# Feed-forward products of a two-layer decoder step in blocks of seven products for eight

## The reference, cut to what matters

```
x += (gelu(causal_dwconv3(h2 @ w_u)) * (h2 @ w_g)) @ w_down,   h2 = RMSNorm(x)
D_MODEL = 1024, FFN_DIM = 2816, CONV_W = 3
w_up: (DEPTH, 1024, 2 * 2816) holds w_u and w_g; w_down: (DEPTH, 2816, 1024)
```

## Time and profile before

| | |
|---|---|
| runs | 2318.37, 2318.27 and 2322.32 us, median 2318.37 |
| profiled execution | span 2314.9 us, from the first to the last instruction; the page gives no time around the span |
| busy in the span | PE 98%, PE weight loads 79%, VectorE 35%, ScalarE 20%, GpSimd 7% |
| granted clock of PE | 0.994 of full, mean |
| feed-forward stage of layer 0 | from 669.83 to 1159.6 us; of layer 1 from 1815.9 us to the end |
| transfers | 237.50 MB, mean 103 GB/s |

### The profile page before, as it was taken

How to read it: one execution, slowest core, us unless ns; L and a number is a source line. 1 busy time by engine, 2 the same in 40 slices (tenths; PEclk the granted TensorE clock), 3 DMA queues, 4 the chain that set the end, 5 groups by cost and what they waited for, 6 DMA issues and landing times.

```text
span 2314.9 us, 29844 instructions
## 1 busy us (share of the span) xinstructions
PE 2266.4 (98%) x12615; PEld 1821.0 (79%) x12615; DVE 815.3 (35%) x1860; ACT 455.2 (20%) x957; POOL 154.9 (7%) x245
## 2 busy tenths in 40 slices
PE   8998999999999999999999989999999999999999
PEld 7787776788888888888877867767888888888887
DVE  5566646444133222100026565574421322222000
ACT  2123135321011111110012231354101111111000
POOL 5140010010000000000021300100100000000000
PEclk9999999999999999999999999999999999999999
DMA  6674621112222222222384726111222212222222
GB/s 181 220 247 164 243 85 37 37 59 93 76 73 73 73 73 70 64 53 68 81 275 129 258 92 273 55 37 37 96 73 76 73 63 68 70 73 64 66 75 76
DMA packets 195081, 237.50 MB, mean 103 GB/s; under 512 B 39807, under 2 KB 174464, under 8 KB 192192
## 3 DMA queue, kind: packets, MB, share of 16 engines
q1 hardware_dynamic: 176104, 133.11, 19.4%
q0 software_dynamic: 18400, 102.36, 11.9%
q10 hardware_dynamic: 444, 0.12, 0.0%
HBM read 222.76 MB, written 21.11 MB: 105 GB/s over the span
## 4 chain that ended last, share of the span: by engine, by line
PE 91%; DVE 3%; DMA 2%; ACT 2%; issue 1%; another core or an unknown queue 1%; SPq 0%; POOL 0%; DVEq 0%; ACTq 0%; POOLq 0%
PE PS L814 51%; PE PS L1455 14%; PE PS L926 5%; PE PS L836 4%; PE PS L862 3%; PE PS L1260 2%; PE PS L1177 2%; PE PS L1188 2%; PE PS L414 2%; DMA arena<-in_cache_kv_slc_dram,idx 2%; ACT arena L1486 1%; PE PS L1135 1%; DVE arena L2143 1%; PE PS L1160 1%
## 5 line engine op out<-in xcount | busy, mean ns | idle before, releaser
L814 PE MATMUL PS<-hT,ring 128*128 128x272 f32 x4352 | 1013.4, 395 | 5.8 <-issue 2.9
L814 PEld LDWEIGHTS PS<-hT,ring 128*128 128x128 f32 x4352 | 828.0, 191 | 185.1 <-issue 15.1
L1486 ACT ACTIVATE arena<-PS 128x512 f32<-128x512 f32 (+13 forms) x307 | 135.2, 475 | 1082.9 <-PE PS L814 559.8
L1455 PE MATMUL PS<-arena,ring 128*128 128x272 f32 x1408 | 323.7, 392 | 0.0
L1455 PEld LDWEIGHTS PS<-arena,ring 128*128 128x128 f32 x1408 | 267.2, 190 | 54.8
L1812 DVE TENSOR_TENSOR arena<-PS,arena 128x544 f32<-128x544 f32 (+3 forms) x124 | 75.4, 618 | 376.6 <-PE PS L814 319.1
L814 PE MATMUL PS<-arena,ring 128*128 128x272 f32 x768 | 177.2, 393 | 3.1 <-DVE arena L1812 3.1
L1818 DVE SCALAR_TENSOR_TENSOR arena<-arena,prm 128x32 f32<-128x32 f32 (+1 forms) x176 | 88.0, 500 | 249.2 <-ACT arena L1486 245.9
L814 PEld LDWEIGHTS PS<-arena,ring 128*128 128x128 f32 x768 | 145.8, 190 | 33.9 <-DVE arena L1812 4.0
L1812 DVE TENSOR_TENSOR xT<-PS,xT 128x544 f32<-128x544 f32 x32 | 23.2, 725 | 386.2 <-PE PS L1455 303.2
L836 PE MATMUL PS<-ring,hT 128*128 128x256 f32 x640 | 142.2, 381 | 0.6 <-ACT qT L1486 0.6
(11 more groups left out here) (311 smaller groups left out, 1620.5 us busy)
## 6 DMA issues: line engine op xcount, KB each, us to landing
ring<-in_w_up_dram SPq DMA_DIRECT2D x88, 512.0 KB, 4.1
ring<-in_w_in_dram SPq DMA_DIRECT2D x68, 512.0 KB, 4.7
ring<-in_w_down_dram SPq DMA_DIRECT2D x32, 384.0 KB, 3.6
ring<-in_w_down_dram SPq DMA_DIRECT2D x32, 320.0 KB, 4.3
arena<-in_state_kv_win_dram POOLq DMA_DIRECT2D x4, 2048.0 KB
ring<-in_w_out_dram SPq DMA_DIRECT2D x16, 512.0 KB, 4.3
out_dram<-in_state_kv_win_dram POOLq DMA_DIRECT2D x2, 4064.0 KB, 40.0
ring<-in_w_in_dram SPq DMA_DIRECT2D x16, 256.0 KB, 6.5
```

The costliest lines, as they stand in the source:

```text
L814: mm = pe.matmul(PS[0:m, b + a, 0:HALF], weight(k), rhs(k)[:, HALF * a:HALF * a + HALF], start=(k == 0), stop=(k == nk - 1))
L1455: mm = pe.matmul(PS[:, b + a, 0:HALF], w[:, k, :], aT[:, 11 * half + k, HALF * a:HALF * a + HALF], start=(half == 0 and k == 0), stop=(hal ...
L1486: return nc.scalar.activation(out, in_, func, **kw)
```

## The change

The matrix products of up/gate steps 1 to 10 and of the whole down stage are cut into blocks of 2 x 2: the input features in two halves (of 4 row blocks; in the last part of down of 3), the output features in two chunks of 128, the tokens in two halves of 272. Such a block took eight products of a quarter of the weights with a quarter of the tokens; now it takes seven, each of 4 (or 3) matmuls of 272 tokens. Four sums of weight quarters and four of token quarters are made on VectorE: the weight sums for every block (`weight_sum`, into `sums` and, one of them, in place in the ring), the token sums of `hT` once a layer (`hsum`, over the place of `raw`), those of `aT` once per pair of row blocks (`asum`, in the strips that attention and convolution have left free).

The seven products add onto each other in PSUM. Bank x of the first ticket is a running sum that is read four times (after its 1st, 2nd, 3rd and last product), bank z of the second ticket twice, bank z+1 once. TensorE waits (`taken`) before it adds onto a bank whose value is still to be read. In the up/gate loop ScalarE copies four partial results (`take`, `take_last`) and VectorE adds three (`add_seven`); in the down stage VectorE adds all seven to `xT`. The centre tap is now made from `ue`, and the gate is multiplied in from `aT`. The down stage runs in three parts over the hidden features (8, 8 and 6 row blocks), each over four pairs of output chunks, so that each pair of `xT` is added to three times. The last two chunks of the output are turned and stored together (before: the last alone).

```diff
+DOWN = [(8 * part, min(8, FC - 8 * part) // 2, pair) for part in range(3) for pair in range(KC // 2)]
+SEVENS = [f"{kind}{i}" for i in range(1, FFN // WCOLS) for kind in "ug"] + [f"d{n}" for n in range(len(DOWN))]
...
+            def half_product(bank, weight, rhs, kc, start, stop):
+
+                for k in range(kc):
+                    mm = pe.matmul(PS[:, bank, 0:HALF], weight[:, k, :], rhs(k), start=(start and k == 0), stop=(stop and k == kc - 1), skip_group_check=not start)
+                return mm
+
+            def seven_products(name, pool, first, second, kc, top, low, right, t1, t2, t3, t4, taken, between=None):
+
+                n, s = SEVEN_AT[name], wload(name)
+                new = sums[n % 2][:, :, 0:kc, :]
+                pe.wait_ge(*S.claim(pe, pool, first))
+                x = S.banks(pe, first)
+                half_product(x, quarter(s, kc, 0, 0), top, kc, True, True).then_inc(*S.inc(pe, "part"))
+                pe.wait_ge(*S.claim(pe, pool, second))
+                z = S.banks(pe, second)
+                pe.wait_ge(*S.at(pe, "w_sum", 4 * n + 1))
+                pe.wait_ge(*t1[0])
+                half_product(z, new[:, 0], t1[1], kc, True, True).then_inc(*S.inc(pe, "part"))
+                pe.wait_ge(*taken[0])
+                pe.wait_ge(*S.at(pe, "w_sum", 4 * n + 3))
+                pe.wait_ge(*t2[0])
+                half_product(x, new[:, 1], t2[1], kc, False, True).then_inc(*S.inc(pe, "part"))
+                half_product(z + 1, quarter(s, kc, 1, 0), low, kc, True, True).then_inc(*S.inc(pe, "part"))
+                pe.wait_ge(*taken[2])
+                pe.wait_ge(*t3[0])
+                half_product(x, quarter(s, kc, 0, 1), t3[1], kc, False, True).then_inc(*S.inc(pe, "part"))
+                pe.wait_ge(*taken[1])
+                pe.wait_ge(*S.at(pe, "w_sum", 4 * n + 4))
+                half_product(z, new[:, 2], right, kc, False, True).then_inc(*S.fill(pe, second))
+                if between:
+                    between()
+                pe.wait_ge(*taken[3])
...
+            def down_seven(n, between):
+
+                first, kc, _ = DOWN[n]
+                j0, whole = 4 * (n // 4), S.at(pe, "a_sum", 4 * (4 * (n // 4) + kc))
+                taken = [S.at(pe, "added", 4 * n + i + 1) for i in range(4)]
+                pe.wait_ge(*S.at(pe, "aT", first + 2 * kc))
+                seven_products(f"d{n}", down_pool(n), f"dx{n}", f"dz{n}", kc, lambda k: ahalf(j0 + k, 0, 0), lambda k: ahalf(j0 + k, 1, 0), lambda k: ahalf(j0 + k, 1, 1),
+                               (whole, lambda k: asum[j0 + k][0]), (whole, lambda k: asum[j0 + k][1]),
+                               (whole, lambda k: ahalf(j0 + k, 0, 1)), (whole, lambda k: asum[j0 + k][2]), taken, between)
 
...
-                        raw_products(("u0", "u1"), s, "n2", (0, 6), 0, 1)
-                    else:
-                        for c in range(2):
-                            fm("T", f"u{2 * i + c}", s, P * c)
-                    s = wload(f"g{i}")
+                    if i:
+                        h_seven(f"u{i}", "T", f"u{2 * i}", f"u{2 * i + 1}")
+                        h_seven(f"g{i}", "S", f"g{2 * i}", f"g{2 * i + 1}")
+                        continue
+                    raw_products(("u0", "u1"), wload("u0"), "n2", (0, 6), 0, 1)
+                    s = wload("g0")
...
+                def take(n, i, ticket, out):
+
+                    act.wait_ge(*S.at(act, "part", 5 * n + i + 1))
+                    run(out, PS[:, S.banks(act, ticket), 0:HALF], ACT.Copy).then_inc(*S.inc(act, "copied"))
+
...
+                for c in range(2):
+                    act.wait_ge(*S.drained(act, f"u{c}"))
+                    run(acc[c], ue[c][:, 2:546], ACT.Identity, scale=gm(PR_WCONV + 44 + c), bias=gm(PR_BCONV + c)).then_inc(*S.inc(act, "acc"))
+                for c in range(2):
+                    gelu(c)
+                for i in range(1, FFN // WCOLS):
+                    c, nu, ng = 2 * i, SEVEN_AT[f"u{i}"], SEVEN_AT[f"g{i}"]
+                    act.wait_ge(*S.at(act, "ue_free", c - 1))
+                    take(nu, 0, f"u{c}", ue[0][:, 2:2 + HALF])
+                    act.wait_ge(*S.at(act, "ue_free", c))
+                    take(nu, 1, f"u{c + 1}", ue[1][:, 2 + HALF:2 + NT])
+                    take(nu, 2, f"u{c}", ue[0][:, 2 + HALF:2 + NT])
+                    act.wait_ge(*S.drained(act, f"u{c + 1}"))
+                    center(c)
+                    take_last(f"u{c}", ue[1][:, 2:2 + HALF])
+                    act.wait_ge(*S.drained(act, f"u{c}"))
+                    act.wait_ge(*S.at(act, "met", nu + 1))
+                    center(c + 1)
+                    take(ng, 0, f"g{c}", aT[:, c, 0:HALF])
+                    take(ng, 1, f"g{c + 1}", aT[:, c + 1, HALF:NT])
+                    gelu(c)
+                    take(ng, 2, f"g{c}", aT[:, c, HALF:NT])
+                    gelu(c + 1)
+                    take_last(f"g{c}", aT[:, c + 1, 0:HALF])
...
+                def weight_sum(name, step):
+
+                    n, s = SEVEN_AT[name], wslot(name)[0]
+                    kc = DOWN[int(name[1:])][1] if name[0] == "d" else 4
+                    new = sums[n % 2][:, :, 0:kc, :]
+                    if step == 0:
+                        dv.wait_ge(*w_landed(dv, name))
+                        tt(new[:, 0], quarter(s, kc, 0, 1), quarter(s, kc, 1, 1), ALU.add).then_inc(*S.inc(dv, "w_sum"))
+                    if step == 1:
+                        tt(quarter(s, kc, 0, 1), quarter(s, kc, 0, 0), quarter(s, kc, 0, 1), ALU.subtract).then_inc(*S.inc(dv, "w_sum"))
+                    if step == 2:
+                        dv.wait_ge(*S.at(dv, "w_sum", 4 * n + 1))
+                        tt(new[:, 1], new[:, 0], quarter(s, kc, 0, 0), ALU.subtract).then_inc(*S.inc(dv, "w_sum"))
+                    if step == 3:
+                        dv.wait_ge(*S.at(dv, "w_sum", 4 * n + 3))
+                        tt(new[:, 2], quarter(s, kc, 1, 0), new[:, 1], ALU.subtract).then_inc(*S.inc(dv, "w_sum"))
+
+                def weight_sums(name):
+
+                    n = SEVEN_AT[name]
+                    if n >= 2:
+                        dv.wait_ge(*S.filled(dv, last_ticket(SEVENS[n - 2])))
+                    for step in range(4):
+                        weight_sum(name, step)
...
+                def add_seven(name, first, second, d0, d1):
+
+                    n = SEVEN_AT[name]
+                    z = S.banks(dv, second)
+                    dv.wait_ge(*S.at(dv, "part", 5 * n + 4))
+                    dv.wait_ge(*S.at(dv, "copied", 3 * n + 1))
+                    tt(d0[:, 0:HALF], PS[:, z + 1, 0:HALF], d0[:, 0:HALF], ALU.add).then_inc(*S.inc(dv, "dve_step"))
+                    dv.wait_ge(*S.at(dv, "part", 5 * n + 5))
+                    dv.wait_ge(*S.at(dv, "copied", 3 * n + 2))
+                    tt(d1[:, HALF:NT], PS[:, S.banks(dv, first), 0:HALF], d1[:, HALF:NT], ALU.add).then_inc(*S.inc(dv, "met"))
+                    dv.wait_ge(*S.filled(dv, second))
+                    dv.wait_ge(*S.at(dv, "copied", 3 * n + 3))
+                    tt(d0[:, HALF:NT], PS[:, z, 0:HALF], d0[:, HALF:NT], ALU.add).then_inc(*S.drain(dv, second))
+
+                dv.wait_ge(*S.at(dv, "h_ready", 2 * KC))
...
+                tt(hsum[:, 0], low[:, :, HALF:NT], low[:, :, 0:HALF], ALU.subtract).then_inc(*S.inc(dv, "h_sum"))
+                dv.wait_ge(*S.at(dv, "h_sum", 1))
+                tt(hsum[:, 1], high[:, :, HALF:NT], hsum[:, 0], ALU.subtract).then_inc(*S.inc(dv, "h_sum"))
+                tt(hsum[:, 2], high[:, :, HALF:NT], low[:, :, HALF:NT], ALU.subtract).then_inc(*S.inc(dv, "h_sum"))
+                dv.wait_ge(*S.at(dv, "h_sum", 2))
+                tt(hsum[:, 3], high[:, :, 0:HALF], hsum[:, 1], ALU.subtract).then_inc(*S.inc(dv, "h_sum"))
                 for q in range(3):
                     n = min(8, FC - 8 * q)
...
+                weight_sums("u1")
+                for c in range(2):
+                    conv(c)
+                for c in range(2):
+                    dv.wait_ge(*S.at(dv, "gelu", c + 1))
+                    dv.wait_ge(*S.filled(dv, f"g{c}"))
+                    b = S.banks(dv, f"g{c}")
+                    tt(two(aT[:, c, :]), pair2(b), two(acc[c % 2]), ALU.mult).then_inc(*S.drain(dv, f"g{c}"))
+                    dv.wait_ge(*S.drained(dv, f"g{c}"))
+                    dv.nop().then_inc(*S.inc(dv, "aT"))
+                for i in range(1, FFN // WCOLS):
+                    c = 2 * i
+                    if i > 1:
+                        gated(c - 1)
+                    weight_sums(f"g{i}")
+                    add_seven(f"u{i}", f"u{c}", f"u{c + 1}", ue[0][:, 2:2 + NT], ue[1][:, 2:2 + NT])
+                    conv(c)
+                    conv(c + 1)
+                    weight_sums(f"u{i + 1}" if i + 1 < FFN // WCOLS else "d0")
+                    if 4 <= i < 8:
+                        for step in range(4):
+                            token_sum(i - 4, step)
```

(13 more changed lines are left out.)

262 lines of the change are left out of this document (157 added, 105 removed).

## The result

| kernel | median us (lowest to highest) | runs | span profiled | TensorE busy | idle | instructions |
|---|---|---|---|---|---|---|
| before | 2320.35 (2318.27 to 2323.03) | 4 | 2314.9 | 2266.4 | 48.5 | 12615 |
| after | 2218.6 (2215.23 to 2221.93) | 4 | 2217.7 | 2159.4 | 58.3 | 12119 |

The ratio is 0.9559 [0.9539, 0.9579]: 4.4% faster, 2218.6 us where 2219.4 was predicted. Busy fell by 107.0 us, idle grew by 9.8. It gives 11.3 us before and 15.7 after, so that without it busy fell by 111.4.

What follows compares the result with a forecast made beforehand. TensorE's instruction count was taken as the bound: span 2314.9 - 113.7 (instructions) + 10.2 (first-block waits) + 3.4 (clock) + 1.1 (end) = 2215.9, plus 3.5 from span to median, 2219.4 us; range 2205 to 2242.

Steps and rivals of the forecast that it cites:

- Instructions: Up/gate and down blocks: seven products for eight, 496 fewer TensorE instructions at 0.2292 us, 113.7 us saved.
- Same bank eight times, and product switches: Inside the new products: eight instructions on one bank taken at 0, up to 11 us; switches possibly 158 us.
- Rival C: Blocks of seven: each of 448 product switches exposes the pipeline for 0.35 us, 158 us in all, 2377 us; 3%.
- The first block: Once a layer TensorE's third product waits 5.1 us for ScalarE's copy behind sums, convolutions and gelus; 10.2 us in all.
- Its clock: Behind the first block's wait: 0.5 to 5.8 us of work at half pace, taken as 1.7 us a layer, 3.4 us.
- VectorE's unseen sizes: Durations estimated from nearby rows: half add 0.42 us, 128x512 sum 0.61, token sum of 1088 1.28, ScalarE copy 0.40.
- rival B: Steady steps: with VectorE sums at 1.0 us the gate's adds come late, up to 52 us, typically 2245 us; 15%.
- The steady steps: Up/gate steps after the first block: at least 1.2 us of slack everywhere, so sums and copies cost nothing.
- Rival D: Between products: small waits make the clock fall again and again, +796 us if it never rose, 3015 us; 1%.
- nothing again: Down blocks: VectorE's work between products, 1.75 us against 1.83 (0.9 against 1.38 with six rows), costs TensorE no wait.
- The end: Kernel's end: last group with two column chunks and a store of 512 KB in place of 256 KB adds 1.1 us.
- The 3.5 us carried from span to median: Whole kernel: the median before lay 3.5 us above its profiled span; added to the predicted span of 2215.9, giving 2219.4.

Runs made afterwards that it cites:

- eight_products: Changed kernel with one product of each block made a second time onto its bank, so eight again: 2327.04 us, 1.0086 of the kernel before.
- Both experiments on it: Changed kernel with first weight sums ahead of the transposed conv-state copies: ratio 0.9542; then also ScalarE's first half-product copy ahead of the two gelus: 0.9522 of before.
- sums_twice: Changed kernel with three of the four weight sums of each block made twice: 2219.93 us, 0.9627 of the kernel before.
- no_sums: Changed kernel without weight and token sums, products reading plain quarters instead, output wrong: 2200.81 us, 0.955 of the kernel before.
- After_again: The changed kernel unaltered, run on another chip as the measure for runs there: 2207.21 us, 0.9568 of the kernel before.
- sums_first: Changed kernel with the first block's weight sums made ahead of the copies of the transposed conv state: 2198.67 us, 0.9542 of the kernel before.
- up_gate_only: Seven products only in up/gate steps 1 to 10, down stage and layer turn as in the kernel before: 2242.99 us, 0.972 of before.

## Why the prediction was right

**Instructions.** 496 fewer at 229.2 ns, -113.7 us: confirmed by the count, by blocks of 12.83 us in up/gate and down (9.62 us between 1078.61 and 1088.23 with six rows; 12.8 and 9.6 were predicted) and, the other way round, by eight_products.

**Same bank eight times, and product switches.** Taken at 0, up to 11 and 158 us held possible. Seven products of eight instructions come at the same 229.2 ns as the two long groups of before, so neither shows a price: in up/gate and down, 0 was right. The token-major products still take 14.0 us for 64:

```profile
1170.27 14.08 PE L866 MATMUL PS<-ring,hT 128*128 128x256 f32 x64
1184.28 1.05 PE L978 MATMUL PS<-arena,fold 128*32 128x512 f32 x2
```

Their excess over 215.7 ns is therefore their own and not the bank's. Rival C is out.

**The first block.** Predicted 5.1 us a layer by VectorE's sums, convolutions and ScalarE's order; the third product came 4.97 us late (715.93, against 707.29 + 3.67), with the sums at 2.54 us where 2.56 was counted. Both experiments on it took away the part that they should. Its clock was put at 1.7 us a layer and cost 2.3 in layer 0 (the two products behind the wait took 3.79 and 2.19 us, not 1.83 each) and 1.8 in layer 1. The bounds of 0.5 and 5.8 us of slow work were not worked out from the rows; twice the cost, 4.6 and 3.6 us, lies inside them.

**VectorE's unseen sizes.** The half add was taken at 0.42 and is 0.44, the sum at 0.61 and starts every 0.60 to 0.61, the token sums of 1088 at 1.28 and are 1.29, ScalarE's copy 0.40 and is 0.40: the views of 128 elements in steps cost nothing extra, and with that rival B went. The Trainium skill (VectorE: DVE Perf Modes, section The TRN2 errata — SBUF-src ops pay a fixed extra latency per instruction) gives (N + 151)/0.96 ns for an fp32 add, checked there for 512 and 2048 elements; for 272, 512 and 1088 that is, as an estimate, 441, 691 and 1291 ns, and the trace agrees: 0.44, 0.69 and 1.28 to 1.29 us.

**The steady steps.** No wait in them, as predicted, and the slack was of the predicted size: three more sums make a block's sums 2.17 us longer (799.62 to 804.33 in sums_twice, 2.54 us in the changed kernel). At 2.17 plain steps still held and at 4.34 they waited 1.21, so their slack is near 3.1 us (an estimate); steps with token sums waited 0.56 at 2.17 and 2.8 at 4.34, so theirs is near 1.6. "At least 1.2" stood in the prediction.

**The clock between blocks.** 1.00 over 248 us of blocks with a product switch every 1.83 us. Rival D, and the depth-cycling that the Trainium skill describes (TensorE: Matmul & The Clock Gate, section A second HAM failure mode: psum-queue depth-cycling), did not occur here: the engine never went idle at a switch. One reason given against D was nevertheless wrong, that it took an idle stretch of 3.76 us to bring a fall. The trace of the kernel before has a fall behind two waits of 1.88 and 1.04 us (1184 to 1192, below) and one with TensorE busy throughout (1642 to 1646), and no_sums has one behind 2.31 us. D is out because the blocks have no waits, not because short waits are harmless.

**What was missed.** At the layers' turn the last two down blocks claim the same PSUM pool one after the other, and the next stage claims it again: the products at 1106.89 and 1117.34 came 0.8 and 0.7 us late. That is most of the 2.0 us that down gave less in layer 0. The "nothing again" of the down blocks was wrong there: it looked at the sums and adds inside a block, not at the claims between the last blocks. What the prediction called hidden at this turn, the sum of squares, was hidden (the products at 1122.91 follow without a wait). The end was sized at 1.1 and cost 0.8.

**Luck in the last step.** The span was predicted at 2215.9 and is 2217.7, 1.8 too low, where the first block's clock (0.7 us more than its 3.4) and the layers' turn (1.5) are the terms that came out larger. The 3.5 us carried from span to median were 1.7 too high: every run whose own span is on record, of whichever kernel, lies 1.7 to 1.8 above it. The 3.5 were taken from a profiled execution whose span of 2314.9 plus 1.8 is none of the three runs of before, so it was probably a fourth. The two errors cancel, so the agreement of 2219.4 with 2218.6 is closer than the working deserves.

**What is not the change's.** Two stages where nothing changed moved by +5.4 and -5.5. In layer 0 the clock fell in 498 to 506 with TensorE busy throughout, which by the estimate cost 3.4 of the 5.4 us; at 214 to 222 it cost 1.1 more than before:

```profile
496.00:498.00 2.00, 2.00 (x38) 1.77 (x34) 0.99 (x2) 0.00 (x0) 0.00 (x0) 1.00 0.00 0
498.00:500.00 2.00, 2.00 (x28) 2.00 (x26) 1.09 (x2) 0.00 (x0) 0.00 (x0) 0.64 0.03 8
500.00:504.00 4.00, 4.00 (x14) 2.86 (x11) 0.69 (x1) 0.00 (x0) 2.11 (x3) 0.50 0.14 44
```

In layer 1 it was the kernel before that had falls, at 1184 to 1192 (3.0 us), behind these waits, and at 1642 to 1646 (1.7 us), without a wait:

```profile
1184.66 0.39 PE L814 MATMUL PS<-hT,ring 128*128 128x272 f32 x1 [1.88 <-issue]
1186.09 10.09 PE L814 MATMUL PS<-hT,ring 128*128 128x272 f32 x31 [1.04 <-issue]
```

The changed kernel had no fall at either place and waited 1.6 us in all where before waited 2.9. After_again, the same kernel on another chip, has none of these waits, so they are not the change's. The two stages cancel by luck; with the first alone the span would have been some 7 us above the predicted one, still inside the range.

## What to carry to other kernels

Where TensorE sets the time at a steady pace per instruction, seven products for eight are worth their count of instructions times that pace, as long as each handoff inside the block meets its due time; extra VectorE work is free up to a slack of a definite size and then costs in full, so count each handoff's due time in the tightest step and not the engine's load. The cost of such a change sits where the pipeline starts: look for a queue in which the first reader of a new result stands behind work that is not urgent, since reordering two queues there gave another 0.5%. A later saving should be compared as busy and idle time apart, because falls of the clock in stages that nobody touched cost 1.5 to 3.4 us each and, with short waits beside them, moved two of them by 5 us.

## What the hardware showed unexpectedly

A wait of 2.21 us left the clock at 1.00 (sums_first) while one of 2.31 (no_sums, the row below) was followed by 0.50, and waits of 1.2 us never were. In the kernel before, waits of 1.88 and 1.04 us close together had a fall with them. From so few cases it stays open whether the length decided or the moment.

```profile
698.99 16.24 PE L899 MATMUL PS<-hT,ring 128*128 128x272 f32 x63 [2.31 <-ACT arena L1547]
```

The clock also fell where TensorE was busy: at 490 to 506 in eight of the eleven traces behind "before", among small products of the attention, and at 1642 to 1650 in two traces (before and eight_products). No_sums, sums_twice and up_gate_only, whose attention is the same program, have none at 490 to 506. What sets that off was not tried. The three chips of the experiments put the kernel before at medians of 2303, 2309 and 2305 us, against 2320 where the prediction was made; the ratio of the changed kernel was the same on the three chips where it ran, within its interval (0.9559, 0.9568, 0.9559).
